# Row scale and gain of the FFN norm moved behind the transposes, and the order of splits in front changed, in a one-core hybrid decoder block

## What is computed

```python
merged = (jax.nn.sigmoid(ga) * (y_a @ w_up_a[l]) + jax.nn.sigmoid(gb) * (y_b @ w_up_b[l]))
x = x + merged @ w_out[l]
x = x + moe_ffn(rmsnorm(x, norm_ffn[l]), w_router[l], b_router[l], w_gu[l], b_gu[l], w_down[l], b_down[l])

def moe_ffn(h, ...):                      # 32 experts, 4 for each token
    logits = (xt @ w_router) + b_router
    top_val, top_idx = lax.top_k(logits, TOP_K)
    gates = jax.nn.softmax(top_val, axis=-1)
    ...
    gu = xb @ w_gu[e] + b_gu[e]           # 1024 -> 2048
    act = (lin + 1.0) * gate * jax.nn.sigmoid(SWIGLU_ALPHA * gate)
    return act @ w_down[e] + b_down[e]    # 1024 -> 1024
```

## Time and profile before

| | |
|---|---|
| three runs | 1169.27, 1171.42, 1173.53 us; median 1171.42 |
| profiled execution | 1167.93 us, its span 1166.1 us |
| busy: TensorE, VectorE, ScalarE, GpSimd | 1135.3, 318.0, 207.8, 20.5 us |
| granted TensorE clock | 0.999 of full |
| moved by DMA | 443.47 MB, 380 GB/s over the span |

### The profile page before, as it was taken

The page is one execution under the profiler, slowest core; times in us unless marked ns, Lnnn a source line. Parts: engine busy times, 40 slices in busy tenths (PEclk is TensorE's granted clock), DMA queues, the critical chain, the costliest instruction groups (busy, mean ns, idle before and its releaser), DMA issues.

```text
span 1166.1 us, 14703 instructions
## 1 busy us (share of the span) xinstructions
PE 1135.3 (97%) x5940; PEld 498.8 (43%) x5940; DVE 318.0 (27%) x560; ACT 207.8 (18%) x291; POOL 20.5 (2%) x25
## 2 busy tenths in 40 slices
PE   9999999999999999999999999999999999999997
PEld 6898999553333333333333333333333333223332
DVE  5688755241111221111111111111111111111112
ACT  3554333010101111101011111101010101010102
POOL 0020002000000000000000000000000000000000
PEclk9999999999999999999999999999999999999999
DMA  9966436969999999999999999999999999999994
GB/s 305 244 208 251 160 143 244 371 265 416 430 429 427 429 429 428 428 429 428 428 429 428 429 429 428 429 429 426 430 429 427 430 429 427 430 429 427 430 426 181
DMA packets 47757, 443.47 MB, mean 380 GB/s; under 512 B 4568, under 2 KB 8184, under 8 KB 23160
## 3 DMA queue, kind: packets, MB, share of 16 engines
q1 hardware_dynamic: 45960, 439.13, 91.4%
q10 hardware_dynamic: 1776, 4.04, 1.0%
HBM read 441.71 MB, written 1.44 MB: 380 GB/s over the span
## 4 chain that ended last, share of the span: by engine, by line
PE 67%; DMA 24%; DVE 5%; ACT 2%; SPq 1%; issue 1%; POOL 0%; POOLq 0%; DVEq 0%; ACTq 0%
PE psum L883 25%; DMA ring<-in_w_gu 17%; PE psum L921 16%; PE psum L840 4%; DMA ring<-in_w_down 4%; PE psum L855 4%; DMA ring<-in_w_in 2%; PE psum L813 2%; DVE slot_r L1173 2%; PE psum L894 2%; PE psum L536 1%; PE psum L543 1%; PE psum L538 1%; PE psum L849 1%; PE psum L905 1%
## 5 line engine op out<-in xcount | busy, mean ns | idle before, releaser
L883 PE MATMUL psum<-ring,hT_region 128*64 128x512 f32 x1280 | 289.6, 594 | 12.3 <-DMA ring<-in_w_gu 12.3
L921 PE MATMUL psum<-ring,hT_region 128*64 128x512 f32 x768 | 175.4, 598 | 2.7 <-DMA ring<-in_w_down 2.7
L883 PEld LDWEIGHTS psum<-ring,hT_region 128*64 128x64 f32 x1280 | 89.6, 137 | 201.7 <-issue 176.5
L1458 DVE TENSOR_SCALAR hT_region<-psum 128x512 f32<-128x512 f32 x32 | 22.1, 692 | 400.9 <-PE psum L883 400.9
L1108 ACT ACTIVATE va_region<-hT_region 128x512 f32<-128x512 f32 x32 | 20.1, 629 | 418.9 <-DVE hT_region L1458 418.9
L921 PEld LDWEIGHTS psum<-ring,hT_region 128*64 128x64 f32 x768 | 50.9, 136 | 93.0 <-issue 89.9
L1452 DVE TENSOR_SCALAR idx_region<-cst,tiny 128x128 f32 x64 | 19.6, 345 | 194.6 <-PE psum L921 192.9
L840 PE MATMUL psum<-work,idx_region 128*64 128x512 f32 x264 | 71.0, 617 | 0.1
L1173 DVE TENSOR_TENSOR slot_r<-ring,slot_r 128x2048 fp32r<-128x2048 f32 (+1 forms) x21 | 61.4, 2931 | 33.0 <-ACT slot_r L969 18.3
L855 PE MATMUL psum<-x_sb,idx_region 64*128 64x512 f32 x264 | 65.6, 615 | 0.0
L883 PE MATMUL psum<-qk_silu,hT_region 128*64 128x512 f32 x256 | 58.5, 598 | 1.0 <-DMA qk_silu<-in_w_gu 0.9
(11 more groups left out here) (266 smaller groups left out, 1111.6 us busy)
## 6 DMA issues: line engine op xcount, KB each, us to landing
ring<-in_w_gu SPq DMA_DIRECT2D x80, 2048.0 KB, 25.5
ring<-in_w_down SPq DMA_DIRECT2D x48, 2048.0 KB, 21.0
bias_vb<-in_w_gu SPq DMA_DIRECT2D x16, 2048.0 KB, 26.4
qk_silu<-in_w_gu SPq DMA_DIRECT2D x16, 2048.0 KB, 27.2
hg<-in_w_down SPq DMA_DIRECT2D x16, 2048.0 KB, 31.2
sig_ab<-in_w_gu SPq DMA_DIRECT2D x16, 2048.0 KB, 28.8
ring<-in_w_in SPq DMA_DIRECT2D x12, 1024.0 KB, 5.1
ring<-in_w_in SPq DMA_DIRECT2D x5, 2048.0 KB, 14.4
```

What stands on the lines that cost most here:

```text
L883: last = mm(psum[half * 64:half * 64 + 64, b, :], xgT_sb[:, a:a + SLOTS], slot_gu(p, c, b, half)[:, jj], start=(j == 0), stop=(j == NJ - 1 ...
L921: last = mm(psum[half * 64:half * 64 + 64, 2, :], actT_sb[:, a:a + SLOTS], slot4(DOWN_HOME[p][c])[:, k, half * 512:(half + 1) * 512], star ...
L1458: v.tensor_scalar(gate_sb, psum[:, 0, :], LIMIT, None, ALU.min).then_inc(gate_ready, 1)
```

## The change

Four moves in the mixers' part: VectorE's `take_low(2)` behind `w_idx`, TensorE's `logits(0)` behind `project(6, 1)`, ScalarE's `take_high(8, 0)` ahead of the Exps, and both parts of the last half of w_up_b behind y_b's (`take_high(13, 1)`, `take_low(13, 1)`); TensorE's wait for `evacuated[1]` moves to the fifth column block of `up`. The FFN norm is no longer applied to the rows. `h2` takes the plain rows, half of them through ScalarE and half through VectorE. The gain multiplies the router's weights once (`wr3`) and the gathered columns in each item (`rows_to_columns`, on VectorE); the root multiplies the router's sums in `route` and stands in the one-hots `pick`. So ScalarE now copies the rows and VectorE makes the columns. `norm_ffn` is loaded as eight numbers for each partition. Half of the filler products between the two routers go. Item table: items 0 to 31 are written early; the rest is worked out on one partition behind the gates, with no product, and `norm_final`'s load waits for it.

```diff
@@ -256,9 +251,12 @@
...
-        n_over, cum, le = (score[:, S + i * NE:S + (i + 1) * NE] for i in range(3))
-        items = take(4)
-        odd_steps, half_over = le[0:1, 0:MAX_ITEMS // 2 - NE // 2], items[0:1, 3:4]
+        n_over, cum, le = score[:, S:S + NE], score[:, S + NE:S + 2 * NE], score[:, S + 2 * NE:S + 4 * NE]
+        odd_steps, half_over = le[0:1, 0:MAX_ITEMS // 2 - NE // 2], le[0:1, NE - 1:NE]
+        g_ffn = take(NJ)
+        over = MAX_ITEMS - NE + 1
+        over_le = work0[0:1, 256:256 + over * NE].rearrange("p (k e) -> p k e", k=over)
+        over_e, over_before, over_none = (le[0:1, i * over:(i + 1) * over] for i in range(3))
@@ -683,9 +681,9 @@
...
             project(6, 0)
+            project(6, 1)
             pe.wait_ge(logits_ready, 1)
             logits(0)
-            project(6, 1)
             pe.wait_ge(hgrn_ready, 1)
@@ -753,8 +751,9 @@
...
             pe.wait_ge(evacuated[0], len(ORDER) // 2)
-            pe.wait_ge(evacuated[1], len(ORDER) // 2)
             for m in range(NJ):
+                if m == NJ // 2:
+                    pe.wait_ge(evacuated[1], len(ORDER) // 2)
                 last = up(UP_A, m, y_a_high, y_a_low)
@@ -785,18 +784,20 @@
...
                 for j in range(NJ):
-                    if r == 1 and j == 4:
-                        keep_warm(2, 1)
+                    if j == 0:
+                        pe.wait_ge(h2_ready_act, r + 1)
                     if j % 4 == 0:
...
                     last = nc.tensor.transpose(dst[:, j, :], h2[:, r, j, :], ident)
-                last.then_inc(h2T_mm, 1)
+                    if j % 4 == 3:
+                        last.then_inc(h2T_mm, 1)
...
-                pe.wait_ge(router_w_in, 16)
-                pe.wait_ge(h2T_ready[r], 2)
+                pe.wait_ge(wr_ready, 1)
                 for j in range(NJ):
+                    if j % 4 == 0:
+                        pe.wait_ge(h2T_ready_act if j else h2T_ready, r + 1)
                     last = mm(psum[:, 2 * r, 0:NE], h2T[:, j, r * P:(r + 1) * P],
@@ -819,9 +820,8 @@
...
             router(0)
-            keep_warm(5, 1)
             h2_transposes(1)
-            keep_warm(3, 1)
+            keep_warm(2, 1)
             router(1)
@@ -855,18 +855,16 @@
...
+            pe.wait_ge(pick0_ready, 1)
+            gather(0)
...
-            gather(0)
...
-            keep_warm(1, 0)
-            pe.wait_ge(items_ready, 1)
-            mm(psum[0:1, 2, 0:P], items[:, 0:1], ident, start=True, stop=True)
-            mm(psum[0:1, 2, P:2 * P], items[:, 1:2], ident, start=True, stop=True).then_inc(items_mm, 1)
+            keep_warm(2, 0)
@@ -1013,6 +1011,7 @@
...
             f(hf, proj(5), ACT.Sigmoid).then_inc(evacuated[1], 1)
+            take_high(8, 0)
             for n, r in enumerate((1, 0)):
@@ -1021,7 +1020,6 @@
...
             f(vb_region, proj(6), ACT.Copy).then_inc(evacuated[0], 1)
-            take_high(8, 0)
             take_high(8, 1)
@@ -1046,7 +1044,7 @@
...
             f(y_a_high, banks(4, 6), ACT.Copy).then_inc(ya_ready, 1)
-            act.dma_start(va_region[:, :], norm_ffn[0].partition_broadcast(P)).then_inc(ffn_gain_in, 16)
+            act.dma_start(g_ffn, norm_ffn[0].rearrange("(p j) -> p j", j=NJ)).then_inc(ffn_gain_in, 16)
             chunk_done(9)
@@ -1061,9 +1059,9 @@
...
             f(sig_b[:, 1024:2048], proj(11), ACT.Sigmoid).then_inc(evacuated[1], 1)
-            take_high(13, 1)
             act.wait_ge(yb_ready, 1)
             f(y_b_high, hf, ACT.Copy).then_inc(y_b_high_ready, 1)
+            take_high(13, 1)
             f(ident_r, ident, ACT.Copy).then_inc(x_high_ready, 1)
@@ -1075,29 +1073,33 @@
...
             def copy_h2T(r):
-                act.wait_ge(h2T_mm, r + 1)
+                act.wait_ge(h2T_mm, 2 * r + 2)
                 f(h2T[:, 4:8, r * P:(r + 1) * P], psum[:, 2 * r + 1, :].rearrange("p (j t) -> p j t", j=4),
-                  ACT.Copy).then_inc(h2T_ready[r], 1)
+                  ACT.Copy).then_inc(h2T_ready_act, 1)
...
                 act.wait_ge(out_mm, n + 1)
+                if n % 2 == 0:
+                    f(h2[:, n // 2, :, 0:64], psum[:, 4 + n, :].rearrange("p (q j) -> p j q", j=NJ),
+                      ACT.Copy).then_inc(h2_ready_act, 1)
+                else:
+                    act.wait_ge(h2_ready, n + 1)
                 if n:
...
             copy_h2T(1)
+            act.wait_ge(xg_mm, 1)
+            f(xg_sb, psum[:, 3, :], ACT.Copy).then_inc(xg_rows_ready, 1)
             act.wait_ge(router_max, NT)
...
             last.then_inc(router_exp, 1)
-            act.wait_ge(xg_mm, 1)
-            f(xg_sb, psum[:, 3, :], ACT.Copy).then_inc(xg_rows_ready, 1)
-            act.wait_ge(gather_mm, 1)
-            f(xgT_sb, psum[:, 3, :], ACT.Copy).then_inc(xg_ready, 1)
             act.wait_ge(gates_ready, 1)
+            act.wait_ge(table_ready, 1)
             act.dma_start(final_gain, norm_final.partition_broadcast(P)).then_inc(final_gain_in, 16)
@@ -1110,8 +1112,8 @@
...
                 f(combT_sb, psum[:, 0, 0:NT * P], ACT.Copy).then_inc(combT_ready, 1)
-                act.wait_ge(gather_mm, i + 2)
-                f(xgT_sb, psum[:, 3, :], ACT.Copy).then_inc(xg_ready, 1)
+                act.wait_ge(xg_mm, i + 2)
+                f(xg_sb, psum[:, 3, :], ACT.Copy).then_inc(xg_rows_ready, 1)
                 act.wait_ge(y_mm, i + 2)
@@ -1207,10 +1209,10 @@
...
-            take_low(2)
             dve.wait_ge(wT_mm, 1)
...
                             ALU.mult).then_inc(evacuated[0], 1)
+            take_low(2)
             dve.wait_ge(evacuated[0], 1)
@@ -1325,7 +1327,6 @@
...
             take_low(13, 0)
-            take_low(13, 1)
             dve.wait_ge(yb_mm, 1)
@@ -1345,6 +1346,8 @@
...
                 v.tensor_tensor(sig_a[:, cols], psum[:, b, :], sig_a[:, cols], ALU.mult).then_inc(up_a_ready, 1)
+                if b == 0:
+                    take_low(13, 1)
             dve.wait_ge(up_a_ready, NJ // 2)
@@ -1354,19 +1357,16 @@
...
-
-            def norm_ffn_half(r, half):
-
-                tiles = slice(4 * half, 4 * half + 4)
-                stream = banks(4 + 2 * r, 6 + 2 * r).rearrange("p (q j) -> p j q", j=NJ)
-                gain = va_region[:, :].rearrange("p (q j) -> p j q", j=NJ)
-                v.scalar_tensor_tensor(h2[:, r, tiles], stream[:, tiles], rs[:, r:r + 1], gain[:, tiles],
-                                       ALU.mult, ALU.mult).then_inc(h2_ready, 1)
+            dve.wait_ge(router_w_in, 16)
+            wr3 = wr_sb.rearrange("p (j e) -> p j e", j=NJ)
+            v.tensor_tensor(wr3, wr3, bc(g_ffn.unsqueeze(2), [P, NJ, NE]), ALU.mult).then_inc(wr_ready, 1)
...
-                link(v.tensor_tensor(r_logits[:, r, :], psum[:, 2 * r, 0:NE], router_b, ALU.add))
+                dve.wait_ge(rs_ready, NT + r + 1)
+                link(v.scalar_tensor_tensor(r_logits[:, r, :], psum[:, 2 * r, 0:NE], rs[:, r:r + 1], router_b,
+                                            ALU.mult, ALU.add))
@@ -1376,13 +1376,26 @@
...
-            for r in range(NT):
-                dve.wait_ge(rs_ready, NT + r + 1)
-                norm_ffn_half(r, 0)
-                norm_ffn_half(r, 1)
-                dve.wait_ge(h2T_mm, r + 1)
+            v.tensor_copy(table[0:1, 0:NE], iota[0:1, 0:NE])
+            v.memset(table[0:1, TAB:TAB + NE], 0)
+
+            def rows_out(r):
+
+                dve.wait_ge(out_mm, 2 * r + 2)
+                stream = psum[:, 5 + 2 * r, :].rearrange("p (q j) -> p j q", j=NJ)
+                for tiles in (slice(0, 4), slice(4, 8)):
+                    v.tensor_copy(h2[:, r, tiles, 64:128], stream[:, tiles]).then_inc(h2_ready, 1)
+
+            def copy_h2T(r):
+
+                dve.wait_ge(h2T_mm, 2 * r + 1)
...
-                              psum[:, 2 * r, :].rearrange("p (j t) -> p j t", j=4)).then_inc(h2T_ready[r], 1)
+                              psum[:, 2 * r, :].rearrange("p (j t) -> p j t", j=4)).then_inc(h2T_ready, 1)
+
+            rows_out(0)
+            copy_h2T(0)
+            rows_out(1)
+            copy_h2T(1)
@@ -1391,9 +1404,13 @@
...
-            for r in range(NT):
-                last = v.tensor_scalar(pick[:, r, :], iota[:, 0:SLOTS], pos[:, r, 0:1], None, ALU.is_equal)
-            last.then_inc(pick_ready, 1)
+            def first_pick(r):
+
+                return v.tensor_scalar(pick[:, r, :], iota[:, 0:SLOTS], pos[:, r, 0:1], rs[:, r:r + 1], ALU.is_equal,
+                                       ALU.mult)
+
+            first_pick(0).then_inc(pick0_ready, 1)
+            first_pick(1).then_inc(pick_ready, 1)
@@ -1404,22 +1421,17 @@
...
-            link(v.tensor_scalar(le, cum, over_idx, None, ALU.is_le))
-            link(v.tensor_reduce(items[:, 0:1], le, AX.X, ALU.add))
-            link(v.tensor_tensor(le, le, cum, ALU.mult))
-            link(v.tensor_reduce(items[:, 2:3], le, AX.X, ALU.max))
-            link(v.tensor_scalar(items[:, 3:4], items[:, 0:1], float(NE), float(S // SLOTS), ALU.is_equal, ALU.mult))
```

(56 more changed lines are left out.)

6 lines of the change are left out of this document (3 added, 3 removed).

## The result

| | before | after |
|---|---|---|
| runs, median | 1170.79 us (1169.27 to 1173.53) | 1162.55 us (1161.46 to 1163.36) |
| ratio, with its 95% interval | | 0.9928 (0.9914 to 0.9942) |
| ratio in a second comparison, five rounds | | 0.9943 (0.9928 to 0.9957) |
| profiled execution, its span | 1167.93, 1166.1 us | 1161.87, 1160.0 us |
| busy: TensorE, VectorE, ScalarE, GpSimd | 1135.3, 318.0, 207.8, 20.5 us | 1132.0, 321.4, 204.7, 20.7 us |

The change makes the kernel faster by 0.7%. Profile against profile it is 1167.93 - 1161.87 = 6.06 us, the 6.1 of the sum. Median against median it is 8.2 us; in the second comparison the ratio gives 0.57% of 1170.6, which is 6.7, and the medians 7.6.

A forecast was written before the change was run, and what follows sets the result against it. The weight stream's restart plus a fixed number of bytes sets the end. Item 0 was to start 4.6 + 2.8 = 7.4 us earlier, with 1.3 given back: -6.1, so 1165.3 from the median 1171.42; own range 1163 to 1168, wide 1162.5 to 1169.5.

The forecast's parts named there:

- the sum: Whole kernel: item 0 starts 7.4 us earlier, 1.3 is given back behind it, so the end comes 6.1 us earlier.
- the projections: Four places where TensorE stands, up to the second `up`: together 4.6 us gained.
- router to item 0: From the output projection's end to item 0, rows copied unnormed: about 2.8 us gained, ends 1.8 and 3.1.
- (a): `take_low(2)` behind `w_idx`: TensorE's 1.09 us wait goes, but a later wait for `hgrn_ready` leaves only about 0.44.
- (b): `take_high(8, 0)` ahead of the Exps: probability transposes at 115.8 instead of 119.00, 3.2 us together with (a)'s 0.44.
- (c): TensorE asks for `evacuated[1]` only at the fifth column block of `up`: about 0.3 us gained.
- (d): y_b's gain and copy go ahead of w_up_b's last piece, so the second `up` waits less: 1.1 us gained.
- The term given back: Behind item 0's start: a TensorE stand of about 1.1 us and `norm_final`'s 1.2 share one gap, +1.3 (0.9 to 2.4).
- The step that failed: From profile to median: the runs' median, 3.5 us above the profiled execution, was to gain the same, giving 1165.3.
- rival 4: TensorE's clock falls to 1.2 GHz between router and first release: +12 - 6.1, 1177 us; chance 0.03.
- Rival 3: Each item's new hand-over is late; beyond 4.2 us of cover TensorE rules all 32 items: 1175 us; chance 0.04.
- Rivals 1, 2 and 5: In order: less reaches item 0, 1168.5 (0.17); item 0 holds the stream, 1170.0 (0.08); more is gained, 1164.0 (0.10).

The follow-up runs named there:

- ffn_only: The changed kernel with the projections' part back in the order of before; ratio 0.9983 to the kernel before, span 1168.3 us.
- without_high8: The kernel after with only ScalarE's `take_high(8, 0)` put back behind the Exps; ratio 0.9981 to the kernel before, median 1168.49 us.
- the two filled ones: The kernel before with filler products at TensorE's stand: seven ahead of the second level product (0.9991), or nine there and three ahead of the transposes (0.9996).
- mixer_moves_only: The kernel before with only the moves up to the second `up`, FFN norm and item table as before; ratio 0.9951, span 1160.7 us.
- look_high8: One more profiled execution of high8_only, with nothing changed; span 1162.7 us, item 0 at 251.20.
- high8_only: The kernel before with only `take_high(8, 0)` moved ahead of the Exps; ratio 0.9969, span 1165.0 us in its first profiled execution.
- norm_early: The kernel after with the table's scratch row moved, so `norm_final`'s load need not wait for the table; ratio 0.9930 to before, span 1160.4 us.
- the filled order: The kernel before with nine filler products ahead of the second level product and three ahead of the transposes; ratio 0.9996, median 1168.90 us.

## Why the prediction came out as it did

- **The sum held.** Item 0 was forecast 7.4 earlier and came 7.36 earlier (254.23 to 246.87); the projections gave 4.7 (197.09 to 192.40) for 4.6; router to item 0 2.7 for 2.8; the whole 6.06 for 6.1.
- **(a)** As forecast, the wait moved to `diagonal`: 0.66 is left of 1.09, and its products begin at 98.97 instead of 99.34, 0.37 earlier for 0.44.
- **(b)** As forecast, 115.89 for 115.8. The table load in the open cost nothing: the division at 111.94 needs only the first eight Exps, which end at 107.2, so 4.7 us of cover were left.
- **(c), (d)** The transposes ahead of the first `up` begin 3.16 us earlier, the first `up` 3.61 (184.41 to 180.80) and the second 4.69: (c) gave 0.45 for 0.3, (d) 1.1 for 1.1.
- **The term given back** was 1.3. From restart to end four executions with the table behind item 0 take 909.0 to 909.7 us (after twice, `ffn_only`, `without_high8`), mean 909.4; the five of before, the two filled ones, `mixer_moves_only` and `look_high8` take 907.5 to 908.7, mean 908.0: 1.35. The first execution of `high8_only`, with 909.9, is left out of this mean; with it the difference is 1.2. The two parts of this term do share one gap, as `norm_early` showed. On the table load the rows decide: it begins at 245.31, where the copy ahead of it ends, and the first Exp begins at 246.60, where it ends. The 2.66 with a drain of the Trainium skill, ScalarE: Activation LUTs, What ACT_TABLE_LOAD costs, was not paid, only the 1.28 of the load.
- **The step that failed** is the last of the sum, "the same change from it gives 1165.3". It took the 3.5 us between the profiled execution and the median for scatter that both kernels have. Part of them belongs to the order that the change removes. It goes back to one sentence of rival 4: that the clock is 1.00 "also around the stand of 1.86 us". That was read from one execution, and in four others of the same kernel it is not so. Against their mean span of 1167.6 the kernel after (1160.0, 1159.8) is 7.7 shorter, in line with the 8.2 and 7.6 between the medians. So 6.1 is the sum and about 1.5 belongs to executions in which the clock fell, 1.3 of it before item 0. The mean clocks of the 62 runs say the same of the runs without a profile: 5.7 at a full clock, and 2.1 that go with a lower one. What stays open is whether all of the 2.1 is lost behind this stand, since the mean has no place, and the filled order lowered the median by 2.0 but not the ratio.
- **Rival 4** looked for the clock in the wrong place, between router and first release, where it stayed at 1.00 throughout, and with the wrong sign: fewer stands, more clock.
- **Rival 3** had a wrong point of decision. Of its 4.2 us of cover the 1.8 of the late pace are not there in each item: the loop has 16 to 20 us in all, 0.5 to 0.6 per item. The other 2.4, VectorE's under TensorE's own work, were not tested. The error did no harm only because the change adds no time to TensorE's items; that is luck.
- **Rivals 1, 2 and 5** are excluded: the whole gain reached item 0, a pass costs 0.70, and the stand was 1.13, not none. Rival 5 named the time nearest to the measured one, for a reason that did not occur.

## What to carry to other kernels

Before you scale a sum from one profiled execution to a median, ask which of its stretches may run otherwise in other executions: a stand of TensorE that cost 1.9 + 0.56 us here cost about 1.5 more in most of them, because the clock fell behind it. If each run has its mean clock on record, sort the runs by it first. Take the cover of a loop from the sum of its waits over the whole loop (15.9 us here, where 16 to 20 were found), not from the difference between two paces times the number of turns (58). A byte taken out of a full stream is worth nothing if a release holds the next load.

## What the chip showed that was not expected

- The same order with the same stand has the granted clock at 1.00 in one execution and at 0.83 over the ten microseconds from 114 to 124 in four others; in one execution it fell with a stand of 0.46 and one of 0.56 there.
- ScalarE's table load appears where nothing hides it any more: the same load lay under a wait at 86 us, and at 101.88 in the open when `take_high(8, 0)` was put ahead of it.
- Two executions of one kernel, with item 0 at the same time within 0.04 us and the same GB/s in the windows, ended 2.3 us apart (`high8_only`, `look_high8`). They part before 560 us, at loads of w_down; why is open.
